# A compact layout for a chunked delta-rule recurrence, and a wide convolution of few tokens by products over overlapping windows, in a one-core decoder kernel

## The chip, the cores and the metric

One core of a Trainium2 chip runs the whole program in one launch. The metric is the device time of that launch in microseconds. The comparison is between the kernel before and the kernel after one change, on the same inputs.

## What is computed

One layer of a hybrid decoder for 512 prompt tokens and 8 samples of 4 tokens (544 columns in all), width 1024, everything in float32: a gated FFN, a mixer with four groups of 256 channels, and a second FFN. Two of the mixer's groups matter here.

```python
# group B: GLU, then a causal depthwise convolution of width 31, LayerNorm, swish
b_conv = causal_dwconv(b_val * sigmoid(b_gate), conv_b, W['b_conv_w'])
# group C (4 heads of 64): delta-rule recurrence over tokens
sa = einsum('bhij,bhj->bhi', S, -kk_t)
S  = S * w_t + sa[..., None] * (kk_t * a_t) + v_t[..., None] * k_t
y_t = einsum('bhij,bhj->bhi', S, r_t)
```

## The kernel before

The activations lie features by tokens. Every large product is three TensorE products of 32-bit halves (`product`, L298 to L308). Its weights come by DMA through SyncE, are split into a high part by ScalarE (`split_hi`, L280) and a low part by VectorE (`split_lo`, L287, the operation of L289). FFN 1 comes first, then the mixer (19 input column blocks, the recurrence, 8 output blocks), then FFN 2. All five engines run programs written out by hand; the order on an engine is the order of the code, and semaphores join them.

**The recurrence.** The 512 prompt tokens are taken in four tiles of 128 (t = 0 to 3), each of two chunks of 64 tokens (c = 0, 1). There are two pairs of heads (p = 0, 1) with two heads each (h = 0, 1). Within a chunk the recurrence becomes the solution of a unit triangular system of 64 x 64 per head, and its inverse is built by doubling blocks of 1, 2, 4, 8, 16, 32 (`LEVELS`). A tile has 13 stages s (`NSTAGE`):

- s = 0: transposes of keys and values (L1118, L1119), taken out by ScalarE into `bv` (L1229).
- s = 1: products of keys with queries and the removal vectors (L1146), for both heads into separate banks. VectorE cuts them by masks into `nib` (L1295), adds the identity (L1299), takes level 0 into `tt_[..,1]` (L1302), and makes `akb` (L1304) and `rbk` (L1305).
- s = 2: transposes of level 0 (L1126), taken out by ScalarE (L1231).
- odd s from 3 to 11: the product `nib` x `tt_` (L1131), masked by VectorE into `xx` (L1310).
- even s from 4 to 12: products of `tt_` with `xx` (L1137 and L1138; at s = 12 only L1138), taken out by ScalarE into `tt_` (L1233) or, at s = 12, into `tf` (L1235). An odd and an even stage are called a level here.

Before the change the two chunks of a tile stand side by side: each of these matrices is 128 x 128 per head, of which only the two diagonal blocks of 64 x 64 are not zero (the product of `akb`, L1157, uses the off-diagonal ones). TensorE multiplies whole 128 x 128 matrices.

Beside a tile t's stages run the seven hops of tile t - 1 (`HOPS`, `chain_pe`: L1173, L1178, L1189, L1198, L1213, L1216), which carry the state from chunk to chunk, and by `BESIDE` the samples' steps q0 to q9, x0, x1 (L1351, L1377, L1404, L1526), splits w2 and w3 of output weights, splits y0 to y3 of the mixer's outputs, and the LayerNorm of group B (b_mean L1415, b_var L1423). PSUM banks 0 to 3 go round as a ring of two pairs (`RING`, `freed`): a stage may write when the stage two places earlier has been read. Behind tile 0's q0 and tile 1's q7 this makes the next stage wait for `rbk` of s = 1.

**The wide convolution.** VectorE does it as 62 taps (31 taps k for two blocks p of channels, `tap`, L975 to L985): one operation of 512 columns for the prompt (L984) and one of 32 for the samples (L985), each adding to `yb`. `fill(n)` (L1759) does the next n taps. It stands behind each input block from m = 15 to 20 (2 taps each) and behind the VectorE part of the odd stages (3 taps each in tile 0, 2 in the others) until the 62 are used up, which is at s = 7 of tile 3. b_mean waits for all taps.

**Start.** ScalarE issues the constants' DMA (`con`, L2017) and two small ones behind it, and waits for all three (L2020) before its squares of x (L436), on which FFN 1's norm rests.

## Time and profile before

| | us |
|---|---|
| median of 3 runs | 1198.92 |
| the three runs | 1193.13, 1198.92, 1202.80 |
| the profiled execution, device time | 1198.65 |
| its span, first to last instruction | 1196.9 |
| TensorE / VectorE / ScalarE / GpSimd busy in it | 1139.4 / 626.6 / 337.0 / 40.7 |
| constants' DMA | 1158.5 KB |

Busy time of TensorE is from a modelled end of each matmul, so 95% busy is not 95% of its peak. Each float32 product of the recurrence is recorded as two matmuls with a weight load each, so an "x8" in a row is four products. In rows of the time line, instructions of one form that follow each other are merged: start, duration from the first's start to the last's end, engine and line, shapes, count, and in brackets the idle time before it with what ended it. TensorE's clock has two levels, 2.4 GHz (shown as 1.00) and 1.2 GHz (0.50).

### The profile page before, as it was taken

To read this page: it belongs to the slowest core of one execution; us is meant where nothing else is said; L and a number is where in the kernel's file an instruction comes from. 1 tells how busy PE (TensorE), PEld (TensorE's weight loads), DVE (VectorE), ACT (ScalarE), POOL (GpSimd) and SP (SyncE) were. 2 spreads that over 40 slices of the span, in tenths; PEclk is the share of its full clock that TensorE was granted. 3 is DMA by queue.
4 is the path that set the end of the run, shared out by engine and by line. 5 is a ranking of instruction groups with operands and counts; after the bars stand their busy time and mean duration, and the time that the engine had idled before them with its cause. 6 is when DMAs were issued, how large, how long until landed. Compare 5 with 4: busy or idle time off the path is not lost.

```text
span 1196.9 us, 21721 instructions
## 1 busy us (share of the span) xinstructions
PE 1139.4 (95%) x8994; PEld 1116.0 (93%) x8994; DVE 626.6 (52%) x1075; ACT 337.0 (28%) x496; POOL 40.7 (3%) x57
## 2 busy tenths in 40 slices
PE   6999999999999997999898999999999999999996
PEld 6999999999999997998787889989999999999996
DVE  5533343333345875889767616785343443344446
ACT  5321222111213433521234343442122221122221
POOL 0000000000000000210221100000000000000001
PEclk9999999999999988999799998899999999999998
DMA  6313232223222211332501002203233232323222
GB/s 223 113 55 105 89 102 74 88 88 100 76 95 79 74 50 53 77 89 76 41 1 36 1 1 73 57 33 106 80 99 104 70 105 71 106 71 105 70 71 75
DMA packets 35391, 92.23 MB, mean 77 GB/s; under 512 B 10368, under 2 KB 12928, under 8 KB 35200
## 3 DMA queue, kind: packets, MB, share of 16 engines
q1 hardware_dynamic: 34320, 88.78, 23.9%
q10 hardware_dynamic: 1008, 2.56, 0.6%
q8 instruction: 45, 0.74, 0.2%
q14 instruction: 18, 0.15, 0.0%
HBM read 88.05 MB, written 3.28 MB: 76 GB/s over the span
## 4 chain that ended last, share of the span: by engine, by line
PE 81%; DVE 12%; ACT 3%; issue 3%; DMA 1%; DVEq 0%; SPq 0%; ACTq 0%
PE ps L306 71%; DVE wl L289 1%; PE ps L1131 1%; DVE mixf L984 1%; PE ps L1137 1%; PE ps L1138 1%; PE ps L367 1%; DVE a L447 1%; ACT wh L284 1%; DVE tb L676 1%; PE ps L376 1%; DMA x<-in_x 1%; DVE xx L1310 1%; DVE mixf L985 1%; PE ps L1573 1%
## 5 line engine op out<-in xcount | busy, mean ns | idle before, releaser
L306 PE MATMUL ps<-xh,wh 128*128 128x272 f32 x1840 | 404.2, 293 | 22.7 <-DVE wl L289 8.8
L306 PE MATMUL ps<-xh,wl 128*128 128x272 f32 x1840 | 400.7, 291 | 0.0
L306 PE MATMUL ps<-xl,wh 128*128 128x272 f32 x1840 | 399.7, 290 | 0.0
L306 PEld LDWEIGHTS ps<-xh,wh 128*128 128x128 f32 x1840 | 299.6, 191 | 25.2 <-DVE wl L289 15.0
L306 PEld LDWEIGHTS ps<-xl,wh 128*128 128x128 f32 x1840 | 299.7, 191 | 0.0
L306 PEld LDWEIGHTS ps<-xh,wl 128*128 128x128 f32 x1840 | 297.9, 191 | 0.0
L284 ACT ACTIVATE wh<-raw 128x1024 fp32r<-128x1024 f32 (+1 forms) x163 | 167.7, 1032 | 319.5 <-PE ps L306 201.2
L289 DVE TENSOR_TENSOR wl<-raw,wh 128x1024 fp32r<-128x1024 f32 (+1 forms) x163 | 192.5, 1202 | 43.6 <-ACT wh L284 43.3
L306 PE MATMUL ps<-hh,wh 128*128 128x272 f32 x704 | 156.8, 289 | 0.0
L306 PE MATMUL ps<-hh,wl 128*128 128x272 f32 x704 | 155.8, 288 | 0.0
L306 PE MATMUL ps<-hl,wh 128*128 128x272 f32 x704 | 155.6, 288 | 0.0
L797 DVE TENSOR_TENSOR h<-silu,ps 128x544 f32<-128x544 f32 x44 | 31.7, 721 | 210.8 <-PE ps L306 208.9
L306 PEld LDWEIGHTS ps<-hl,wh 128*128 128x128 f32 x704 | 114.5, 189 | 0.0
L306 PEld LDWEIGHTS ps<-hh,wh 128*128 128x128 f32 x704 | 114.3, 189 | 0.0
L306 PEld LDWEIGHTS ps<-hh,wl 128*128 128x128 f32 x704 | 114.2, 189 | 0.0
L783 ACT ACTIVATE silu<-silu 128x544 f32<-128x544 f32 x44 | 29.0, 659 | 231.3 <-DVE silu L793 231.3
L793 DVE TENSOR_TENSOR silu<-ps,rb 128x544 f32<-128x544 f32 x44 | 31.8, 724 | 76.9 <-PE ps L306 73.2
L816 DVE TENSOR_TENSOR f<-ps,f 128x544 f32<-128x544 f32 x24 | 17.4, 724 | 75.5 <-PE ps L306 75.5
L984 DVE SCALAR_TENSOR_TENSOR mixf<-zb,par,mixf 128x512 f32<-128x512 f32 x60 | 44.9, 748 | 0.1
L804 DVE TENSOR_TENSOR hl<-h,hh 128x544 f32 (+1 forms) x44 | 31.9, 726 | 4.3
L813 DVE COPY f<-ps 128x544 f32<-128x544 f32 x16 | 11.6, 724 | 42.7 <-PE ps L306 42.7
L1310 DVE TENSOR_TENSOR xx<-ps,con 128x256 f32<-128x256 f32 x40 | 16.7, 422 | 27.0 <-PE ps L1131 26.6
(311 smaller groups left out, 850.5 us busy)
## 6 DMA issues: line engine op xcount, KB each, us to landing
raw<-in_w_gu SPq DMA_DIRECT2D x88, 512.0 KB, 3.7
raw<-in_w_d SPq DMA_DIRECT2D x32, 512.0 KB, 3.6
raw<-in_w_in SPq DMA_DIRECT2D x19, 512.0 KB, 3.5
raw<-in_w_d SPq DMA_DIRECT2D x16, 384.0 KB, 3.0
raw<-in_w_out SPq DMA_DIRECT2D x8, 512.0 KB, 3.6
out_y<-x SPq DMA_DIRECT2D x16, 136.0 KB, 1.7
con<-in_con ACTq DMA_DIRECT2D x1, 1158.5 KB, 5.1
x<-in_x ACTq DMA_DIRECT2D x4, 272.0 KB, 5.6
```

Source lines behind the costliest of these rows:

```text
L284: act.activation(wh[:, s % 4, 0:k, :], raw[:, s % RAW, 0:k, :], ACT.Copy).then_inc(S("w_hi"), 1 + skip)
L289: dve.tensor_tensor(wl[:, s % 4, 0:k, :], raw[:, s % RAW, 0:k, :], wh[:, s % 4, 0:k, :].bitcast(F32), SUB).then_inc(S("w_lo"), 1 + skip)
L306: last = pe.matmul(out[:, n], left[:, s, j], right[:, j, n * H:n * H + H], start=first and opens and j == order[0], stop=final and closes ...
L367: m = pe.matmul(ps[:, 2 * second + h, 3 * i + j:3 * i + j + 1], a3[:, a_, window(3 * h + j)], ones[:, 0:1], start=True, stop=True)
L376: last = pe.matmul(ps[:, 4 + 2 * second + h, P * j:P * j + wide], src[:, 3 * h + j:3 * h + j + 1].to_broadcast([P, P]), ident[:, P - wide: ...
L783: act.activation(silu[:, s % 2], silu[:, s % 2], ACT.Silu).then_inc(S(f"silu{q}"), 1)
L793: dve.tensor_tensor(halves(silu[:, s % 2]), pair(2 * (s % 2)), halves(rb[:]), MUL).then_inc(S(f"gate{q}"), 1)
L797: dve.tensor_tensor(halves(h32[:, s % 2]), halves(silu[:, s % 2]), pair(2 * (s % 2) + 1), MUL).then_inc(S(f"h_mul{q}"), 1)
L804: dve.tensor_tensor(hl[:, j].rearrange(one), h32[:, s % 2], hh[:, j].rearrange(one).bitcast(F32), SUB).then_inc(S(f"h_lo{q}"), 1)
L816: dve.tensor_tensor(halves(f[:, d]), pair(d % 4), halves(f[:, d]), ADD).then_inc(S(f"d_out{q}"), 1)
L984: eng.scalar_tensor_tensor(y1, z1, w, y1, MUL, ADD)
L1310: dve.tensor_tensor(xx[:, p], done(p)[:, 0:2 * P].rearrange(HC, h=2), C_("lev", k=l * P).unsqueeze(1).to_broadcast([P, 2, P]), MUL).then_i ...
```

## The change

1. `nib`, `akb`, `tt_`, `tf` and `xx` become 128 rows by 64 columns per head: chunk c's block stands in its own 64 partitions. The masks shrink with them (`mask` from 384 to 192 columns, `lev` from 768 to 384).
2. Each 128 x 128 product at L1126, L1131, L1137, L1138 and L1157 becomes two products of 64 x 64, on the quarters of the array in which chunk 0 and chunk 1 lie. The transposes of s = 2 become products with the identity.
3. VectorE and ScalarE work on half the columns at L1310, L1231, L1233 and L1235. At s = 1 the cuts into `nib` and `akb` are two operations each on 64 partitions, the identity and level 0 one operation each in place of two, and both parts of `rbk` come last.
4. The taps no longer touch the samples. Their convolution is 10 operations ("windows"): for each block p and each half of the samples a product of 496 columns (4 samples x 4 tokens x 31 taps, read from `zb` with overlap) and a sum over the 31, and two small additions of the bias. They are put between the last taps.
5. `fill` does 3 in place of 2 for m = 17 to 20 and in tile 1. b_mean waits for the windows too. In all 72 items are done: 16 by m = 20, 18, 18, 12 and 8 in tiles 0 to 3.

```diff
-    c[:, CCOL["mask"]:][:, :P] = (s // C == t // C) & (s < t)
-    c[:, CCOL["mask"] + P:][:, :P] = (s // C != t // C) & (s % C < t % C)
-    c[:, CCOL["mask"] + 2 * P:][:, :P] = s % C <= t % C
+    c[:, CCOL["mask"]:][:, :C] = s % C < t[:, :C]
+    c[:, CCOL["mask"] + C:][:, :P] = s % C <= t % C
...
             if k == 0:
-                eng.tensor_scalar(y1, z1, w, par_("bb", p), MUL, ADD)
-                return eng.tensor_scalar(y2, z2, w, par_("bb", p), MUL, ADD)
-            eng.scalar_tensor_tensor(y1, z1, w, y1, MUL, ADD)
-            return eng.scalar_tensor_tensor(y2, z2, w, y2, MUL, ADD)
+                return eng.tensor_scalar(y1, z1, w, par_("bb", p), MUL, ADD)
+            return eng.scalar_tensor_tensor(y1, z1, w, y1, MUL, ADD)
+
+        wide = tmp2[:, 1, 0:NB // 2 * NT * CONVB].rearrange("p (b t k) -> p b t k", b=NB // 2, k=CONVB)
+
+        def windows(eng, n):
+
+            if n >= 8:
+                return eng.tensor_scalar(yb[:, n - 8, DT], yb[:, n - 8, DT], par_("bb", n - 8), None, ADD)
+            n, what = divmod(n, 2)
+            p, h = divmod(n, 2)
+            if what == 0:
+                z = zb[:, p, 542:].rearrange("p (b c) -> p b c", c=34)[:, 4 * h:4 * h + 4, 0:NT]
+                over = bass.AP(z.tensor, z.offset, [list(d) for d in z.ap] + [[1, CONVB]])
+                w = par[:, PCOL["bw"] + p:PCOL["bw"] + 2 * CONVB:2].unsqueeze(1).unsqueeze(1)
+                return eng.tensor_tensor(wide, over, w.to_broadcast([P, NB // 2, NT, CONVB]), MUL)
+            return eng.tensor_reduce(comp(yb[:, p, DT])[:, 4 * h:4 * h + 4], wide, mybir.AxisListType.X, ADD)
...
                 elif s == 2:
                     b = job(p)
-                    pe.wait_ge(S("tt1"), 2 * t + p + 1)
+                    pe.wait_ge(S("tt1"), t + 1)
                     for h in range(2):
-                        last = pe.transpose(b[:, P * h:P * h + P], tt_[:, p, 1, h], ident)
+                        for c in range(2):
+                            last = pe.matmul(b[hp[c], C * h:C * h + C], tt_[hp[c], p, 1, h], ident[hp[c], C * c:C * c + C],
+                                             start=True, stop=True)
...
                     for h in range(2):
-                        last = pe.matmul(b[:, P * h:P * h + P], nib[:, p, h], tt_[:, p, 0, h], start=True, stop=True)
+                        for c in range(2):
+                            last = pe.matmul(b[hp[c], C * h:C * h + C], nib[hp[c], p, h], tt_[hp[c], p, 0, h], start=True, stop=True)
...
                         if s < 12:
-                            pe.matmul(b[:, P * h:P * h + P], tt_[:, p, 1, h], xx[:, p, h], start=True, stop=True)
-                        last = pe.matmul(b[:, 256 + P * h:256 + P * h + P], xx[:, p, h], tt_[:, p, 1, h], start=True, stop=True)
+                            for c in range(2):
+                                pe.matmul(b[hp[c], C * h:C * h + C], tt_[hp[c], p, 1, h], xx[hp[c], p, h], start=True, stop=True)
+                        for c in range(2):
+                            last = pe.matmul(b[hp[c], P + C * h:P + C * h + C], xx[hp[c], p, h], tt_[hp[c], p, 1, h],
+                                             start=True, stop=True)
...
                         k = P * p + C * h
-                        last = pe.matmul(ps[:, 4 + t % 2, k:k + C], akb[:, p, h], bv[:, t % 2, p, 2, C * h:C * h + C],
-                                         start=k == 0, stop=t == 0, skip_group_check=True)
+                        for c in range(2):
+                            last = pe.matmul(ps[rows(c), 4 + t % 2, k:k + C], akb[hp[c], p, h], bv[hp[c], t % 2, p, 2, C * h:C * h + C],
+                                             start=k == 0, stop=t == 0, skip_group_check=True)
...
-                    act.activation(tt_[:, p].rearrange("p k h c -> p (k h c)"), done(p), ACT.Copy).then_inc(S(f"r{s}"), 1)
+                    act.activation(tt_[:, p].rearrange("p k h c -> p (k h c)"), done(p)[:, 0:2 * P], ACT.Copy).then_inc(S(f"r{s}"), 1)
...
+                for c in range(2):
+                    dve.tensor_tensor(nib[hp[c]].rearrange(hik), own(c, "b"), strict[hp[c]].to_broadcast([64, 2, 2, C]), MUL).then_inc(S("near"), 1)
...
+                dve.tensor_tensor(tt_[:, :, 1], nib[:], C_("lev", C).unsqueeze(1).unsqueeze(1).to_broadcast([P, 2, 2, C]), MUL).then_inc(S("tt1"), 1)
+                for c in range(2):
+                    r = hp[1 - c]
+                    dve.tensor_tensor(akb[r].rearrange(hik), own(c, "k"), strict[r].to_broadcast([64, 2, 2, C]), MUL).then_inc(S("ak"), 1)
...
-                fill(2 if t else 3)
+                fill(2 if t > 1 else 3)
...
-                    dve.tensor_tensor(xx[:, p], done(p)[:, 0:2 * P].rearrange(HC, h=2),
-                                      C_("lev", k=l * P).unsqueeze(1).to_broadcast([P, 2, P]), MUL).then_inc(S(f"r{s}"), 1)
-                fill(2 if t else 3)
+                    dve.tensor_tensor(xx[:, p], done(p)[:, 0:P].rearrange(HC, h=2),
+                                      C_("lev", C, l * C).unsqueeze(1).to_broadcast([P, 2, C]), MUL).then_inc(S(f"r{s}"), 1)
+                fill(2 if t > 1 else 3)
...
+            TAPS = [(k, p) for k in range(CONVB) for p in range(2)]
+            for n in range(10):
+                TAPS.insert(2 * CONVB - 9 + 2 * n, (n, None))
...
-                    fill(2)
+                    fill(2 if m < 17 else 3)
```

## Rows read from the trace of the kernel before

**Rows 1.** The page: engines' busy time; the clock granted to TensorE in 40 slices.
```profile
PE 1139.4 (95%) x8994; PEld 1116.0 (93%) x8994; DVE 626.6 (52%) x1075; ACT 337.0 (28%) x496; POOL 40.7 (3%) x57
...
PEclk9999999999999988999799998899999999999998
```

**Rows 2.** Stretches of tiles 0 to 3: length; PE, PEld, DVE, ACT, POOL busy; clock; DMA; GB/s.
```profile
568.10:605.10 37.00, 31.88 (x266) 27.66 (x267) 27.90 (x74) 8.69 (x20) 8.44 (x9) 0.78 0.44 37
605.10:638.50 33.40, 28.93 (x243) 23.61 (x241) 23.13 (x68) 12.56 (x29) 7.93 (x10) 0.95 0.06 17
638.50:665.00 26.50, 24.48 (x208) 21.72 (x209) 20.02 (x47) 12.63 (x26) 4.01 (x6) 1.00 0.06 21
665.00:696.70 31.70, 28.50 (x240) 25.50 (x238) 16.51 (x41) 12.78 (x27) 3.79 (x6) 1.00 0.00 1
```

**Rows 3.** Time line, tile 3: one level of pair 0.
```profile
685.63 0.67 PE L1131 MATMUL ps<-tt,nib 128*128 128x128 f32 x4
...
688.12 0.60 ACT L1233 ACTIVATE tt<-ps 128x512 f32<-128x512 f32 x1 [1.69 <-PE ps L1138]
...
688.81 0.67 PE L1131 MATMUL ps<-tt,nib 128*128 128x128 f32 x4
```

**Rows 4.** Groups by form, 568 to 697 us (the last is the page's).
```profile
L984 DVE SCALAR_TENSOR_TENSOR mixf<-zb,par,mixf 128x512 f32<-128x512 f32 x52 | 38.9, 749 | 0.0
...
L1131 PE MATMUL ps<-tt,nib 128*128 128x128 f32 x160 | 26.1, 304 | 2.0 <-ACT tt L1233 0.9 <-DVE s0t L1526 0.8 <-DVE qnak L1500 0.2
...
L1233 ACT ACTIVATE tt<-ps 128x512 f32<-128x512 f32 x32 | 19.0, 597 | 33.3 <-PE ps L1138 33.3
L1310 DVE TENSOR_TENSOR xx<-ps,con 128x256 f32<-128x256 f32 x40 | 16.7, 422 | 27.0 <-PE ps L1131 26.6
...
L1235 ACT ACTIVATE tf<-ps 128x256 f32<-128x256 f32 x8 | 2.9, 380 | 6.2 <-PE ps L1138 6.1
...
L793 DVE TENSOR_TENSOR silu<-ps,rb 128x544 f32<-128x544 f32 x44 | 31.8, 724 | 76.9 <-PE ps L306 73.2
```

**Rows 5.** Time line: runs of weight loads and products on the whole array and on parts.
```profile
606.39 0.55 PEld L1146 LDWEIGHTS ps<-ar,bt 64*128 64x128 f32 x8 [1.15 <-DVE qtt L1517]
...
607.51 0.54 PEld L1189 LDWEIGHTS ps<-rhs,tf 64*64 64x64 f32 x8
...
615.71 0.32 PEld L1216 LDWEIGHTS ps<-rbk,uv 128*64 128x64 f32 x8
...
629.87 1.08 PE L1404 MATMUL ps<-qex,qbkv 64*64 64x512 f32 x4
...
678.12 0.97 PEld L1131 LDWEIGHTS ps<-tt,nib 128*128 128x128 f32 x8
```

**Rows 6.** Time line of VectorE: a tap and the start of the next; a sample's tap in tile 0.
```profile
671.57 0.74 DVE L984 SCALAR_TENSOR_TENSOR mixf<-zb,par,mixf 128x512 f32<-128x512 f32 x1
...
672.23 0.24 DVE L985 SCALAR_TENSOR_TENSOR mixf<-zb,par,mixf 128x32 f32<-128x32 f32 x1
672.40 0.74 DVE L984 SCALAR_TENSOR_TENSOR mixf<-zb,par,mixf 128x512 f32<-128x512 f32 x1
...
584.85 1.03 DVE L985 SCALAR_TENSOR_TENSOR mixf<-zb,par,mixf 128x32 f32<-128x32 f32 x1
```

**Rows 7.** Groups at the start: the constants' DMA, and ScalarE's wait for the three.
```profile
con<-in_con ACTq DMA_DIRECT2D x1, 1158.5 KB, 5.1
...
17.69 0.66 ACT L436 ACTIVATE a<-x 128x544 f32<-128x544 f32 x1 [4.06 <-DMA dwbd<-in_dw]
```

**Rows 8.** Time line of TensorE: the first transposes of tile 0.
```profile
568.11 0.69 PE L1118 MATMUL ps<-con,kt 128*128 128x128 f32 x2 [2.83 <-DVE mixf L1831]
```

**Rows 9.** Time line of TensorE, tile 1: s = 2 behind q7.
```profile
610.56 0.44 PE L1126 MATMUL ps<-con,tt 128*128 128x128 f32 x2 [1.03 <-DVE rbk L1305]
```

**Rows 10.** Stretches at 1.2 GHz in the recurrence, first and last of three (columns as in rows 2).
```profile
567.70:577.70 10.00, 7.44 (x38) 4.94 (x38) 7.89 (x21) 2.13 (x5) 0.00 (x0) 0.51 1.00 77
...
611.70:615.10 3.40, 3.40 (x17) 2.85 (x15) 2.53 (x7) 0.92 (x3) 0.00 (x0) 0.50 0.00 0
```

More of the change, by code:

```diff
@@ L68 @@
 _n = 0
-for _name, _k in (("ident", P), ("ones", P), ("hb", P), ("mask", 3 * P), ("lev", 6 * P), ("scan", N), ("cnt", 32),
+for _name, _k in (("ident", P), ("ones", P), ("hb", P), ("mask", C + P), ("lev", 6 * C), ("scan", N), ("cnt", 32),
                   ("wcol", 2), ("eps", 3), ("smask", 64), ("slev", 64), ("bsel", 8), ("idc", 64)):
@@ L1290, in part @@
                     return done(h).rearrange(quads, i=2, c=2, w=2)
-                def mask(n):
-                    return C_("mask", P, n * P).rearrange(HC, h=2).unsqueeze(1).to_broadcast([P, 2, 2, C])
-                for h in range(2):
-                    dve.tensor_tensor(nib[:, :, h].rearrange(ick, c=2), part(h)[:, :, :, 0], mask(0), MUL).then_inc(S("near"), 1)
-                idb = ident.unsqueeze(1).to_broadcast([P, 2, P])
-                for p in range(2):
-                    dve.wait_ge(S("near"), 2 * t + 2)
-                    dve.tensor_tensor(nib[:, p], nib[:, p], idb, ADD).then_inc(S("unit"), 1)
@@ L1300, in wkv_dve @@
-                for p in range(2):
-                    dve.wait_ge(S("unit"), 2 * t + p + 1)
-                    dve.tensor_tensor(tt_[:, p, 1], nib[:, p], C_("lev").unsqueeze(1).to_broadcast([P, 2, P]), MUL).then_inc(S("tt1"), 1)
-                for h in range(2):
-                    dve.tensor_tensor(akb[:, :, h].rearrange(ick, c=2), part(h)[:, :, :, 0], mask(1), MUL).then_inc(S("ak"), 1)
-                    dve.tensor_tensor(rbk[:, t % 2, :, h].rearrange(ick, c=2), part(h)[:, :, :, 1], mask(2), MUL).then_inc(S("r1"), 1)
@@ L1306, in wkv_dve, with own @@
-                fill(2 if t else 3)
+                def own(c, kind):
+                    two = ps[hp[c if kind == "b" else 1 - c], 2 * (place(("r", t, 1)) % 2):2 * (place(("r", t, 1)) % 2) + 2]
+                    return two.rearrange("p h (i c w k) -> p h i c w k", i=2, c=2, w=2)[:, :, :, c, 0]
+                hik = "p i h k -> p h i k"
+                strict = C_("mask", C).unsqueeze(1).unsqueeze(1)
+                upto = C_("mask", P, C).rearrange(HC, h=2).unsqueeze(1).to_broadcast([P, 2, 2, C])
```

42 lines of the change are left out of this document (28 added, 14 removed).

## The prediction

> **What bounds the kernel now.** I began with the page. TensorE is busy in nearly the whole span, and the only slices in which it is granted much less than the full clock lie in the middle [rows 1]. The change touches only that middle (the mixer), and the start through the constants. The split into stretches then gives the four tiles of the recurrence: 37.0, 33.4, 26.5 and 31.7 us, 128.6 together, 11% of the time [rows 2]. VectorE is busy for 27.9 of 37.0 us in tile 0 and 16.5 of 31.7 in tile 3, TensorE for 24.5 of 26.5 in tile 2. So no engine bounds it alone: it is a chain of TensorE, VectorE, TensorE, ScalarE which two pairs of heads share, with taps in front of VectorE's part and hops in front of TensorE's. A quiet level shows the bare chain: from one L1131 of pair 0 to the next 3.18 us (685.63 to 688.81) [rows 3]. It is the product 0.67, the mask 0.42, four products and their latency about 1.05, the copy 0.60, some 0.15 of hand-overs, and 0.27 in which pair 1's L1131 holds TensorE. In the groups, VectorE's idle time before `xx` is put to L1131 (26.6 us), ScalarE's before `tt` to L1138 (33.3 us): each waits for TensorE's products [rows 4].
>
> **The price of a product.** A run of n records of d each that lasts T has a pitch of (T - d)/(n - 1). For L1131 (whole array, 128 columns) that is (0.97 - 0.19)/7 = 0.111 us; for L1189 (one quarter, always the same within a run, 64 columns) (0.54 - 0.135)/7 = 0.058; for L1216 (column halves in turn, 64 columns) (0.32 - 0.135)/7 = 0.03; for L1146 (row halves in turn, 128 columns) (0.55 - 0.19)/7 = 0.05, half of what 128 columns cost otherwise [rows 5]. So column halves work side by side, and row halves too, where they write to different banks. L1404 shows column halves side by side within one bank: four records of 512 columns in 1.08 us [rows 5], where 0.111 x 4 = 0.44 us each, one after another, would be 1.8. The change has neighbours that differ in both, and write to one bank on different partitions. No row of before shows that. The ends are 0.03 and 0.058 us a record; I take 0.03, since both halves of the case are seen overlapping.
>
> The Trainium skill (TensorEngine Tiling, section Restrictions and Gotchas, Gotcha 1) says that different row tiles can't access the same PSUM bank simultaneously. No row of before has that case. By it the quarters would go one by one, and the sum would be the first rival's.
>
> With 0.03: an odd stage (L1131, both pairs) goes from 8 records x 0.111 = 0.89 us to 16 x 0.03 = 0.48, saving 0.41; an even stage from 16 x 0.111 = 1.78 to 32 x 0.03 = 0.96, saving 0.82; L1157 from 0.9 to 0.48, saving about 0.45. The mask falls from 256 to 128 columns: 0.42 for 256 and 0.72 for 544 [rows 4] lie on a line that gives 0.28 for 128 (no less than half, 0.21, no more than 0.42). The copy falls from 512 to 256 columns, 0.60 to 0.38 [rows 4]. A level's chain becomes 0.43 + 0.28 + 0.67 + 0.38 + 0.2 of hand-overs, about 2.0 us, for 3.18.
>
> **Taps.** A tap takes 0.83 us from start to start (671.57 to 672.40), its large part 0.66 of it (to 672.23) [rows 6]. So a tap becomes 0.66. A window's product or sum, 496 columns, isn't in the trace: between 0.33 and 1.3 (half and twice the 0.66 that 496 columns have by the 0.72 for 544 [rows 4]). I take 0.66, by L984 of 512 columns; eight of them lie in tiles 2 and 3, where VectorE has room, so even 1.3 costs at most a few us. Three items and two masks are 2.0 + 0.56 = 2.55 us of VectorE a level (3 x 0.83 + 0.84 = 3.3 before), two items 1.9 (2.5 before).
>
> **The change part by part** (minus is gained):
>
> - Start. The constants shrink by 576 columns, 288 of 1158.5 KB. In proportion to their 5.1 us that is 1.3 us of the wait of 4.06 [rows 7]; with the small DMAs behind it I take -1.0 (0 to -1.3).
> - Input blocks. TensorE's first transposes of tile 0 sit idle for 2.83 us behind VectorE's last block [rows 8]: VectorE sets the end there. m = 16 has two taps, -0.33; m = 17, 18 and 19 have three of 0.66 for two of 0.83, +0.33 each. Sum +0.7.
> - Tile 0, start: s = 1 has 8 VectorE operations for 10 and `rbk`'s first is the seventh for the eighth: -0.35.
> - Tile 0, levels: VectorE bounds s = 3, 9 and 11 at 3.3 us and more; each gives 0.75, -2.3. At s = 5 a sample's tap takes 1.03 us for 0.24 (GpSimd works at that time) [rows 6]; it goes, as one more does: -1.5 (-0.5 to -2.4). At s = 7 TensorE is at 1.2 GHz and bounds the level; products at double price, (0.41 + 0.82) x 2 less what VectorE's 2.55 us put in their place: -2.2. Sum -6.0.
> - Tile 1: the products of s = 2 wait for `rbk` behind q7 [rows 9]; both parts of it come two operations earlier, -0.7. Then TensorE bounds until s = 7: -0.8 (s = 3, at 1.2 GHz), -0.82, -0.45, -0.41, -0.82. From there on VectorE bounds it (split w2, two updates of the samples' state, masks and taps): masks -0.9, taps at 3 x 0.66 for 2 x 0.83 +1.05. Sum -3.85.
> - Tile 2: VectorE lies in front of s = 3 (-0.55 for s = 1's fewer operations, -0.33 for taps). s = 4 gives 0.82 + 0.45, s = 5 and 6 give 0.41 + 0.82. The next two levels fall from 3.2 to 2.6, where VectorE's 1.9 and a split of 0.71 set the end; the last gives 0.8. Sum -5.4.
> - Tile 3: start and s = 3, -0.65 (0.2 of the gain goes to the wait for the state's copy), then -1.27 and -1.23 as before, two bare levels -1.2 each, -0.4 at s = 11. Behind b_mean the LayerNorm of group B is the path and doesn't change. Sum -5.95.
> - Changes between whole array and parts: none is priced by a row. I bound one at nothing and at a weight load's 0.135 to 0.19 us that the next run doesn't hide [rows 5], and take 0.17 for two more a tile in three tiles, +1.0 (0 to +4, at eight a tile).
> - Clock. At present 20 us of the recurrence run at 1.2 GHz, in three stretches of which the first has 10.0 and the last 3.4 us, behind gaps or behind many tiny products [rows 10]. TensorE gets more gaps now. I take one and a half of such short stretches more, each some 1.7 us dearer: +2.5 (-2 to +8 within this case).
>
> Sum: -1.0 + 0.7 - 0.35 - 6.0 - 3.85 - 5.4 - 5.95 + 1.0 + 2.5 = -18.35. From the profiled execution's 1198.65 (span 1196.9 and 1.75 around it; the runs' median is 1198.92) that is 1180.3; I say 1181. This case's own range is 1173 to 1189.
>
> **Rivals.**
>
> *The quarters take turns* (0.058 a record). An odd stage then costs 0.93 us for 0.89, an even one 1.86 for 1.78: TensorE gains nothing. What is left is VectorE's and ScalarE's part: tile 0 -3.9, tile 1 -0.7, tile 2 -1.6, tile 3 -0.45, with start, input blocks and changes of shape +0.7 - 1.0 + 1.0: -5.95, 1193. For it speaks that no row shows two row halves in one bank; against it L1404 and L1146 [rows 5].
>
> *TensorE falls to 1.2 GHz now and again.* Its streaming within a level halves, in levels shortened by a third. In a tile with hops what it has left is about 6.7 us of levels, 5.8 of hops and 2.5 of the rest, 15 us, which at 1.2 GHz become 30. One part in three of tiles 1 to 3 at that clock adds 15, and in place of my 2.5: 1181 + 12.5 = 1194.
>
> *TensorE stays at 1.2 GHz for most of the recurrence: slower.* Place: tiles 1 to 3, TensorE's own part. Price: 3 x 15 = 45 us, tile 0 some 7 more (it is hidden there in part by 2.55 us of VectorE a level), less 3 that VectorE hides in tile 1: about +47 for the 2.5, 1226. It decides the sign once somewhat under half of the tiles is cold. For it speaks that the clock stayed low from 567.7 to 577.7 although TensorE was busy for 7.4 us of the 10 [rows 10], with transposes and row halves among its work. Against it: it came back within 3.4 us in tile 1, where products of whole levels and hops filled it [rows 10], and tiles 2 and 3 stay at 1.00 with TensorE busy for 24.5 of 26.5 us and 28.5 of 31.7 [rows 2]. The Trainium skill (TensorE: Matmul & The Clock Gate, Part 1) has the throttled state as the default, released by activity; the rows on both sides agree, and none of them shows how quarters count.
>
> *The change doesn't save what it says on VectorE:* a product over overlapping windows or a sum at 1.3 us in place of 0.66 adds 8 x 0.64 = 5 us of VectorE in tiles 2 and 3, of which perhaps 3 show: 1184. It lies in the first case's range.
>
> **How the numbers follow.** Likeliest 0.63 (with the last rival in it), turns 0.19, now and again cold 0.12, cold for the most 0.06. One per cent, about what a measurement of this kernel can tell from no change, is 12 us: faster than that is below 1187. Of the likeliest case, 0.85 lies there, of the third about 0.1: 0.55. Above 1211 only the last case: 0.06. The rest, 0.39, is within 1%. The range takes in turns and the middle of the third case: 1173 to 1197; 1 in 10 lies below or just outside the first case, 1 in 10 above.
>
> **What would show it.** Runs of the quarter products of 16 records: a pitch of 0.03 says I am right, 0.058 the first rival. A bare level of 2.0 us from one L1131 of pair 0 to the next in tile 3; 2.9 or 3.2 says no. Tiles of about 30.5, 29.5, 21 and 26 us; the wait for the constants near 3.0 us; TensorE's idle time before tile 0's transposes grown by 0.7. A clock below 1.00 over tiles 2 and 3 would speak for the cold cases. I would be wrong if the levels shortened and the hops took their place as the chain, or if the windows' operations stood in front of `xx`.

## The result, and the profile after

The changed kernel takes 1195.68 us (median of 20 runs, 1190.76 to 1203.65). The kernel before takes 1203.89 us in the same measurement (20 runs, 1193.13 to 1210.77). The ratio is 0.9937, with a 95% interval of 0.9915 to 0.9958: 0.6% faster, about 7.6 us, where 18 were forecast. The profiled execution has a span of 1195.4 us and a device time of 1197.13. That is 1.5 us above the median of its kernel, while the profiled execution of the kernel before (1198.65) is 5.2 us below the median of its own, so whole times are compared here by the runs, and profiles only stretch by stretch. Three later runs that took over 1.5% longer than the fastest of their kernel (two of e3, one of e9) are left out of the ratios and clocks below.

The page, to hold against [rows 1]:

```profile
PEclk9999999999999998999766989889999999999998
```

The recurrence lies in the 20th to 23rd of the 40 slices. The 21st and 22nd (598 to 658 us) stand at 6, where both stood at 9 in the kernel before. The stretches of the four tiles, each from its first transposes to those of the next, the last to the product for b_mean (columns as in rows 2):

```profile
569.60:603.40 33.80, 27.12 (x394) 23.52 (x394) 24.23 (x55) 6.59 (x20) 7.67 (x9) 0.68 0.43 40
603.40:635.00 31.60, 27.39 (x377) 21.27 (x375) 23.63 (x53) 9.84 (x27) 8.73 (x10) 0.72 0.07 18
635.00:663.10 28.10, 25.86 (x343) 21.34 (x342) 17.28 (x42) 11.20 (x28) 4.13 (x6) 0.67 0.07 20
663.10:682.60 19.50, 17.79 (x330) 15.03 (x326) 10.42 (x27) 7.87 (x23) 3.20 (x6) 1.00 0.01 3
```

The bounds in rows 2 were round ones, so here are the same stretches of the kernel before, cut in the same way:

```profile
568.10:604.60 36.50, 31.38 (x262) 27.16 (x262) 27.40 (x73) 8.56 (x20) 8.44 (x9) 0.78 0.45 37
604.60:636.80 32.20, 28.95 (x246) 23.86 (x244) 21.94 (x61) 11.76 (x28) 7.93 (x10) 0.95 0.06 18
636.80:664.90 28.10, 24.86 (x212) 21.87 (x211) 21.62 (x56) 13.53 (x29) 4.01 (x6) 1.00 0.05 20
664.90:690.20 25.30, 23.39 (x204) 20.88 (x203) 14.83 (x39) 9.71 (x23) 3.79 (x6) 1.00 0.01 2
```

Read the last two numbers before the DMA share together with the length. Tile 3 has a granted clock of 1.00 in both kernels and falls from 25.3 to 19.5 us. Tiles 1 and 2 had 0.95 and 1.00 before, have 0.72 and 0.67 now, and give 0.6 us and nothing. Tile 0 went from 0.78 to 0.68 and gives 2.7 us. TensorE is no less busy in tile 2 (25.86 us for 24.86), though the level products that it has there should take about half as long at the full clock: the lower clock took that back.

One level of tile 3, against [rows 3]:

```profile
679.81 0.92 PE L1146 MATMUL ps<-tt,nib 64*64 64x64 f32 x16
...
681.82 0.92 PE L1146 MATMUL ps<-tt,nib 64*64 64x64 f32 x16
```

The bare chain is 2.01 us from one product of a level to the next, for 3.18. A run of weight loads on the diagonal quarters, and the groups, against [rows 4, 5]:

```profile
677.80 0.54 PEld L1146 LDWEIGHTS ps<-tt,nib 64*64 64x64 f32 x16
```

```profile
L1252 ACT ACTIVATE tt<-ps 128x256 f32<-128x256 f32 x32 | 12.2, 384 | 28.7 <-PE ps L1155 27.7
L1337 DVE TENSOR_TENSOR xx<-ps,con 128x128 f32<-128x128 f32 x40 | 10.7, 288 | 26.0 <-PE ps L1146 25.3
L996 DVE TENSOR_TENSOR mixf<-zb,par 128x496 f32<-128x496 f32 x4 | 2.7, 664 | 0.0
L997 DVE TENSOR_REDUCE mixf<-mixf 128x16 f32<-128x496 f32 x4 | 2.6, 656 | 0.0
```

The pitch is (0.54 - 0.135)/15 = 0.027 us. The mask of 128 columns takes 0.288, the copy of 256 takes 0.384, a product or sum over windows 0.66 us. All the prices of instructions are as forecast.

What was not forecast is how long the clock stays low. The two long stretches, and what stands before each on TensorE's time line:

```profile
584.90:615.70 30.80, 30.26 (x343) 26.29 (x342) 19.68 (x47) 7.44 (x23) 4.67 (x6) 0.50 0.01 2
629.50:653.50 24.00, 20.56 (x191) 16.57 (x193) 13.76 (x38) 6.14 (x15) 0.79 (x2) 0.50 0.11 37
```

```profile
585.44 0.58 PE L1369 MATMUL ps<-ar,bt 64*32 64x64 f32 x4 [3.31 <-issue]
...
588.13 5.42 PE L1378 MATMUL ps<-ar,s0t 64*64 64x8 f32 x61
...
631.45 0.98 PE L1146 MATMUL ps<-tt,nib 64*64 64x64 f32 x13 [2.57 <-DVE s0t L1554]
```

TensorE stood still for 3.31 us with no releaser in the profile ("issue"), and then went on at 1.2 GHz for 30.8 us, though it was busy for 30.26 of them. The second stretch begins in a wait of 2.57 us behind VectorE's update of the samples' state. I add up such time from slices of 1 us, as twice what the granted clock lacks to 1: between 560 and 725 us the kernel before has 31 us at 1.2 GHz, the changed one 68. The 20 runs say the same without a trace: their mean granted clock is 0.9515, and that of the kernel before, measured beside e1 and beside e5 below, 0.965 and 0.966. A difference of 0.014 over 1195 us is 2 x 0.014 x 1195 = 33 us more at 1.2 GHz. Measured side by side (e5) the difference is 0.016, or 38 us.

### The profile page after: what moved, and what is told of

Its sections match the earlier page's. It is cut to its first block, busy times and chain, and to the rows that moved or that the text cites. A ratio compares the mean times of both kernels' runs of the same rounds, so it can differ in the third digit from the quotient of the medians.

```text
span 1195.4 us, 22718 instructions
## 1 busy us (share of the span) xinstructions
PE 1134.6 (95%) x9522; PEld 1108.9 (93%) x9522; DVE 617.1 (52%) x1015; ACT 328.9 (28%) x496; POOL 40.3 (3%) x57
## 4 chain that ended last, share of the span: by engine, by line
PE 82%; DVE 11%; issue 3%; ACT 2%; DMA 1%; DVEq 0%; SPq 0%; ACTq 0%
PE ps L306 71%; DVE mixf L982 2%; DVE wl L289 1%; PE ps L1146 1%; PE ps L367 1%; DVE a L447 1%; ACT wh L284 1%; PE ps L376 1%; PE ps L1153 1%; PE ps L1155 1%; DVE tb L676 1%; PE ps L1197 1%; DMA x<-in_x 1%; PE ps L1164 1%; PE ps L1601 1%
## 5 line engine op out<-in xcount | busy, mean ns | idle before, releaser
L306 PE MATMUL ps<-xh,wh 128*128 128x272 f32 x1840 | 405.7, 293 | 22.4 <-DVE wl L289 8.8
L306 PE MATMUL ps<-xh,wl 128*128 128x272 f32 x1840 | 401.9, 292 | 0.0
L306 PE MATMUL ps<-xl,wh 128*128 128x272 f32 x1840 | 400.7, 291 | 0.0
L306 PEld LDWEIGHTS ps<-xh,wh 128*128 128x128 f32 x1840 | 301.5, 192 | 24.9 <-DVE wl L289 14.9
L306 PEld LDWEIGHTS ps<-xl,wh 128*128 128x128 f32 x1840 | 301.1, 192 | 0.0
L306 PEld LDWEIGHTS ps<-xh,wl 128*128 128x128 f32 x1840 | 299.0, 192 | 0.0
L306 PE MATMUL ps<-hh,wh 128*128 128x272 f32 x704 | 156.8, 289 | 0.0
L306 PE MATMUL ps<-hh,wl 128*128 128x272 f32 x704 | 155.7, 288 | 0.0
L306 PE MATMUL ps<-hl,wh 128*128 128x272 f32 x704 | 155.6, 288 | 0.0
L306 PEld LDWEIGHTS ps<-hl,wh 128*128 128x128 f32 x704 | 114.5, 189 | 0.0
L306 PEld LDWEIGHTS ps<-hh,wh 128*128 128x128 f32 x704 | 114.2, 189 | 0.0
L306 PEld LDWEIGHTS ps<-hh,wl 128*128 128x128 f32 x704 | 114.2, 189 | 0.0
L1337 DVE TENSOR_TENSOR xx<-ps,con 128x128 f32<-128x128 f32 x40 | 10.7, 288 | 26.0 <-PE ps L1146 25.3
```

Source lines behind the costliest of these rows:

```text
L306: last = pe.matmul(out[:, n], left[:, s, j], right[:, j, n * H:n * H + H], start=first and opens and j == order[0], stop=final and closes ...
```

## Experiments

"Recurrence" is, in the profiled execution, the time from tile 0's first transposes to the product for b_mean; "cold" is the time at 1.2 GHz between 560 and 725 us, as above. "Clock" is the mean over a kernel's runs, with that of the kernel before, measured beside it, in brackets: read the two together, since the latter alone moves from 0.965 to 0.970. The ratios are to the kernel before on the same chip. Recurrence and cold are of one execution each, and the two profiles of the changed kernel differ by 4.3 us in the first; e3's profiled execution (1214.61 us) is far above the 1201 us that its ratio stands for.

| run | ratio (95% interval) | clock | recurrence | cold |
|---|---|---|---|---|
| before (profile) | 1 | 0.965 to 0.970 | 122.1 | 31 |
| changed (profile) | 0.9937 (0.9915 to 0.9958) | 0.952 | 113.0 | 68 |
| e5, changed, again | 0.9926 (0.9897 to 0.9956) | 0.950 (0.966) | 108.7 | 65 |
| e1 fillers | 0.9893 (0.9831 to 0.9955) | 0.964 (0.965) | 104.5 | 17 |
| e2 stores late | 0.9882 (0.9826 to 0.9938) | 0.950 (0.965) | 111.9 | 75 |
| e3 other order of quarters | 0.9949 (0.9912 to 0.9987) | 0.949 (0.965) | 128.0 | 85 |
| e4 taps only | 1.0017 (0.9985 to 1.0048) | 0.963 (0.965) | 121.7 | 23 |
| e6 fillers, state first | 0.9880 (0.9847 to 0.9913) | 0.965 (0.966) | 110.3 | 34 |
| e7 fillers on before | 1.0051 (1.0026 to 1.0075) | 0.967 (0.966) | 127.9 | 17 |
| e8 compact only | 0.9935 (0.9909 to 0.9962) | 0.950 (0.966) | 106.5 | 48 |
| e9 items moved | 0.9897 (0.9858 to 0.9936) | 0.957 (0.970) | 97.5 | 31 |
| e10 items and fillers | 0.9907 (0.9879 to 0.9935) | 0.966 (0.970) | 108.9 | 31 |
| e11 quarter fillers | 0.9906 (0.9875 to 0.9938) | 0.963 (0.970) | 105.4 | 31 |
| e12 fewer fillers | 0.9841 (0.9805 to 0.9877) | 0.967 (0.970) | 101.1 | 24 |
| e13 items 2, few fillers | 0.9738 (0.9692 to 0.9784) | 0.972 (0.965) | 97.4 | 20 |
| e14 items 2 | 0.9875 (0.9824 to 0.9925) | 0.953 (0.965) | 104.7 | 51 |
| e15 few fillers on before | 0.9977 (0.9948 to 1.0006) | 0.969 (0.965) | 119.6 | 20 |
| e16 items 2, fewest | 0.9781 (0.9730 to 0.9832) | 0.966 (0.965) | 97.4 | 24 |
| e17, e13 again | 0.9763 (0.9713 to 0.9814) | 0.970 (0.965) | 98.1 | 20 |
| e18 and stores late | 0.9775 (0.9726 to 0.9824) | 0.968 (0.965) | 93.8 | 17 |

### Is it the clock, and does it come from the waits?

**e1, fillers.** Products whose result nobody reads, in front of TensorE's work of chosen stages (50 over tiles 0 to 3, and one ahead of each head's products with the samples' state of each pair). They write to a part of a PSUM bank that is not used otherwise.

```diff
+        def fill_pe(pe, n, seen=0):
+            if n and seen > 0:
+                pe.wait_ge(S("y_out"), seen)
+            for _ in range(n):
+                pe.matmul(ps[:, 7, 256:384], ident, con[:, CCOL["lev"]:CCOL["lev"] + P], start=False, stop=True, ...)
...
+            fill_pe(pe, FILLERS.get((t, s), 0), t if s > 6 else max(t - 1, 0))
             for p in range(2):
                 if s == 0:
```

> The kernel after, with useless whole-array products (128 x 128 by 128 columns, into spare columns of bank 7) on TensorE in front of the stages at which it waits: some 35 in tile 0, 20 in tile 1, 6 in tiles 2 and 3, and four within q3. About 60 of 0.22 us are 13 us more work of TensorE, half of it in waits. Clock theory (the missing gain is TensorE at 1.2 GHz for some 60 us of the recurrence, where it was 20): the stretches at 1.2 GHz in 568 to 700 us shrink to under 30 us in sum and the time falls below the kernel after's by 2 to 12 us, to a ratio of 0.980 to 0.992 against before. VectorE theory (taps, split and samples' state on VectorE took the gain, the clock is a side effect): the time is equal to after's or up to 8 us longer, ratio 0.994 to 1.001, even if the clock rises.

Measured 0.9893. The interval from 4 runs reaches from a gain of 0.4% to 1.7%. The profile is clearer: 17 us cold for 68, and tiles 1 and 2 are what they should have been.

```profile
608.90:636.50 27.60, 26.54 (x419) 21.14 (x415) 21.83 (x51) 9.62 (x28) 7.87 (x10) 1.00 0.07 21
636.50:659.00 22.50, 19.89 (x356) 16.52 (x350) 17.95 (x43) 11.31 (x29) 4.13 (x6) 1.00 0.09 26
```

They take 27.6 and 22.5 us for 31.6 and 28.1. Tile 0 didn't shorten (34.9 for 33.8).

**e7, the same fillers on the kernel before**, as the control.

> The kernel before with the same useless products (at the same places of its levels), to see whether they help by themselves. The kernel before has 20 to 31 us at 1.2 GHz between 560 and 725 us. Clock theory: there is little to win back, the products add about 60 records of 0.11 to 0.22 us, partly in waits, so between -0.3% and +0.3%. Rival (such products help any version of this kernel, by filling TensorE in a part where it is throttled anyway): -0.5% or better, as much as they give the changed kernel.

1.0051: they cost the kernel before 0.5%, above what I expected. The changed kernel gains 0.3 to 0.4% by them (e1 against e5 and the first measurement), which alone lies inside the intervals. The two together are 0.9%, with a noise of some 0.7 by the intervals of the runs compared: clear of it, though not by much. So they are no good in themselves; what they win back belongs to the levels of the compact layout.

**e11, quarter fillers.** Each product of the whole array is replaced by two on the diagonal quarters.

```diff
+                for c in range(2):
+                    pe.matmul(ps[hp[c], 7, 256:384], ident[hp[c], C * c:C * c + C], con[hp[c], ...], ...)
```

> The first experiment with each useless whole-array product (two records of about 0.11 us) replaced by two on diagonal quarters, of the same 128 columns, side by side: the same count of places and TensorE busy about as long, with half of the array. If it is TensorE's idle time in the waits that lets the clock fall, these hold it as well as the whole-array ones: 0.989, clock 0.96. If it is the quarters themselves that leave the clock low however busy TensorE is, the clock stays near 0.950 and the ratio at 0.993 or above.

0.9906, in time no different from e1's 0.9893. The clock lies between the two cases: 0.006 below that of the kernel before beside it, for 0.001 in e1 and 0.016 in e5, with 31 us cold. So products on quarters win back over half of the clock, and the shape of the new products isn't all that keeps it down; that it plays some part isn't ruled out.

**e3, the order of the quarters.** Both heads of one chunk, then both of the other; otherwise the changed kernel.

```diff
-                    for h in range(2):
-                        for c in range(2):
+                    for c in range(2):
+                        for h in range(2):
                             last = pe.matmul(b[hp[c], C * h:C * h + C], nib[hp[c], p, h], ...)
```

> The kernel after with the quarter products in another order, all of chunk 0 and then all of chunk 1, so that neighbours within a job mostly use the same quarter. If neighbours on different quarters work side by side and those on the same one take turns, the pitch of the weight loads rises from 0.03 to near 0.058 us, a bare level of tile 3 from 2.0 to about 2.8 us. Clock theory: TensorE is denser and may keep 2.4 GHz longer, so that the time is within 3 us of after's, ratio 0.991 to 0.997. VectorE theory: levels bound by VectorE hide it in tiles 0 and 1, tiles 2 and 3 pay 5 to 8 us, ratio 0.997 to 1.001.

```profile
694.45 0.33 PE L1153 MATMUL ps<-xx,tt 64*64 64x64 f32 x4
694.57 0.33 PE L1154 MATMUL ps<-tt,xx 64*64 64x64 f32 x4
694.74 0.33 PE L1153 MATMUL ps<-xx,tt 64*64 64x64 f32 x4
```

Eight records take 694.74 - 694.45 = 0.29 us, a pitch of 0.036, for 0.029 in the changed kernel. So turning from quarter to quarter with each product is worth only 0.2 us in an even stage; in the odd stages no difference shows (16 loads in 0.59 to 0.60). The pitch of 0.058 that I expected didn't come, and a bare level takes 2.29 us (699.19 to 701.48) where I expected 2.8. This profile also holds the price of the clock, by chance: tile 2 was at 1.2 GHz from end to end.

```profile
642.80:678.40 35.60, 33.65 (x344) 29.10 (x342) 18.37 (x44) 11.51 (x28) 3.72 (x6) 0.50 0.05 16
```

Tile 2 has the same work in the changed kernel and, but for four fillers, in e1. It takes 35.6 us at a clock of 0.50, 28.1 at 0.67 and 22.5 at 1.00. Some 2 us of the first may be the order of the quarters (five even stages of 0.2, doubled at 1.2 GHz), which leaves 11 for a whole tile. In the kernel before the tile took 28.1 us at 1.00. So with two thirds of the tile at 1.2 GHz the loss of 5.6 us is all that the layout gives there.

### Which half of the change gives what?

**e4, the taps alone**: the kernel before with the windows, one large tap an item, and three items a level in tiles 0 and 1. **e8, the compact layout alone**: the changed kernel with the taps and counts of the kernel before.

> The kernel before with only the taps' part of the change: prompt taps of 512 columns alone, the samples by ten window operations, three items in place of two for m = 17 to 20 and in tile 1. By the prediction's steps: input blocks +0.7, tile 0 -1.4 for its VectorE-bound levels and -0.5 to -2.4 at s = 5, tile 1 between 0 and +1, tile 2 -0.33 and the like: 1 to 4 us faster than before, ratio 0.997 to 0.9995. Clock theory: TensorE's stretches at 1.2 GHz are as before's, some 20 us. Should it bring 7 us by itself, the compact layout brings nothing.

> The compact layout alone, with the taps, the samples' convolution and the number of items a level as in the kernel before. My terms for the two halves: the layout carries nearly all of the gain (products, masks, copies), the taps nothing (the converse experiment gave 1.0017). Clock theory: within 0.3% of the changed kernel in this call, ratio 0.991 to 0.997, clock as low as the changed kernel's. Rival (VectorE's items decide in tiles 0 and 1, and the shorter levels only pay with the windows): 0.998 or more.

1.0017 and 0.9935, the latter against 0.9926 for the whole change beside it (**e5**). The taps' part is worth nothing that can be measured (I had expected 0.05 to 0.3%), the layout all of it.

> The changed kernel once more, beside the next three, as their yardstick. In the first measurement its 20 runs had a mean granted clock of 0.9515 and a ratio of 0.9937; I expect the same here, about -0.6% (-7.6 us) against the kernel before, and a clock that is at least 0.010 lower than that of the kernel before in the same call. If the clock of the two kernels is alike in this call, my theory (the clock took what the products gave) falls.

e5 repeats the result, with a clock of 0.950 for the 0.966 of the kernel before. e8, with the layout alone, has 0.950 too.

### What is VectorE's?

**e9, items moved**: the same taps and windows, given out in another order. **e14** takes them out of tile 0's level 5 as well.

```diff
+        ITEMS = [(3, 3, 3, 3, 3, 3), (3, 3, 3, 2, 1, 1), (3, 3, 2, 2, 2, 2), (3, 3, 3, 3, 3, 0)]        # e9
+        ITEMS = [(3, 3, 1, 3, 3, 3), (3, 3, 3, 2, 2, 1), (3, 3, 3, 2, 2, 2), (3, 3, 3, 3, 3, 0)]        # e14
-                fill(2 if t > 1 else 3)
+                fill(ITEMS[t][s // 2])
...
-                    fill(2 if m < 17 else 3)
+                    fill(2)
```

> The changed kernel with VectorE's items given out otherwise: two a step in the input stage (12 for 16), three a level in tile 0, then 3, 3, 3, 2, 1, 1 in tile 1 and 3, 3, 2, 2, 2, 2 in tile 2, and three a level in tile 3 (15 for 8). TensorE's wait before tile 0 (3.52 us behind VectorE's last block) falls by up to 4 x 0.66 = 2.6 us; tile 1, where VectorE bounds the last levels, gives up to 3; tile 3 loses about 2, since three items and two masks are 2.5 us where its bare level is 2.0. Sum -2 to -4 us against the changed kernel, so about 0.990 of the kernel before. Clock theory adds: the clock stays as low as in the changed kernel (0.950). Rival (VectorE's items in tiles 0 and 1 are where the missing 11 us are): 0.985 or better.

> The same order of items without useless products. Against the first order of moved items (0.9897) TensorE's wait of 2.56 us behind the samples' masks in tile 0 goes or falls under 0.5 us: 0.9875. The clock stays between the changed kernel's and the one before: 0.955 to 0.960. Rival (that wait is only filled by the level's own chain, which is late by then too): 0.9897, no change.

0.9897 and 0.9875, as expected. TensorE's wait before tile 0 falls from 3.52 to 1.58 us, and in tile 1 that behind the samples' state from 2.57 to 1.24. e9's profile has 31 us cold for 65 to 68 and e14's has 51, but the runs show little of it: their clocks are 0.012 below that of the kernel before beside them, where e5's was 0.016 below. In e14's profile TensorE's idle time without a releaser stands at 3.35 us, and the clock falls behind it. It took the place of the wait that the moved items were to remove: with one item at level 5 VectorE was through at 584.82 and then stood still for 2.98 us behind TensorE's products.

Why level 5 of tile 0: this is VectorE and GpSimd in the kernel with fewer fillers (e12).

```profile
587.17 3.96 DVE L982 SCALAR_TENSOR_TENSOR mixf<-zb,par,mixf 128x512 f32<-128x512 f32 x3
```

```profile
586.64 3.94 POOL L1513 TENSOR_TENSOR qex<-qbkv,con 32x512 f32<-32x512 f32 x3 [0.18 <-POOL uv L1298]
```

Three taps take 3.96 us beside GpSimd's work, and 2.07 without it (583.53, same kernel). TensorE waited 2.47 us behind them. It isn't the DMA traffic of that time: in e6, where the DMA engines were busy for 0.01 of 585 to 590 us, three taps beside GpSimd took 4.51.

### Do both together reach the forecast?

**e12**, e1 with 32 fillers instead of 54, kept where TensorE waits longest; **e15**, the same set on the kernel before; **e13**, the set with e14's order of items; **e17**, e13 once more; **e16**, as e13 with 18 fillers.

```diff
-        FILLERS = {(0, 2): 6, (1, 2): 1, (2, 2): 4, (3, 2): 2, (0, 3): 1, (0, 4): 2, (0, 5): 4, ...
+        FILLERS = {(0, 2): 6, (0, 5): 4, (0, 6): 1, (0, 8): 1, (0, 10): 1, (0, 12): 1, (1, 2): 1, (1, 9): 3, (1, 11): 8, (2, 2): 4, (3, 2): 2}   # e12, e13, e15, e17, e18
+        FILLERS = {(0, 2): 6, (1, 9): 2, (1, 11): 4, (2, 2): 4, (3, 2): 2}                                                                        # e16
```

> The first experiment with 28 useless products for 50 or so: those in front of the samples' products of their state and in most levels of tiles 0 and 1 are left out, those in the longest waits kept (behind the masks of each tile, tile 0's level 5, tile 1's levels 9 and 11). On the kernel before the full set cost 0.5%, so about a quarter of a per cent is to be saved if the clock holds: 0.987. If the many small ones were what held the clock, it falls to about 0.955 and the ratio is 0.992.

> The smaller set of useless products on the kernel before. They add 28 x 2 records where the full set added some 55 x 2 and cost 0.5%; the kernel before has the better clock already. Clock theory: 0.999 to 1.003. Rival (they help either kernel alike): 0.995 or better.

> The changed kernel with the smaller set of useless products (0.9841 alone) and the items moved again: one item in place of three at tile 0's level 5, where GpSimd's work doubles the time of a tap, the two going to later tiles. Moved items alone gave 0.9897, the products 0.9841, the changed kernel 0.9926 to 0.9937. If waits of VectorE and TensorE's clock are two causes, the gains add: 0.978 to 0.982, and the recurrence takes 96 to 99 us (101.1 and 97.5 us with one of them each). If they are one (fewer waits keep the clock up, and nothing else is lost), it is no better than 0.984.

> As the first of these four with 18 useless products for 28 or so: none in tile 0's levels, two and four in tile 1's levels 9 and 11. If the products pay where TensorE waits longest (behind the masks and behind the samples' state), this is as good as the larger set, within 0.2%; if those in tile 0 matter, its clock falls under 0.962 and it loses 0.3% or more.

> The same kernel as e13_items2_few_fillers once more. If its 0.9738 stands: 0.971 to 0.979, clock 0.970. If it was a lucky draw, it lands at the sum of its parts, 0.9841 and 0.9875 for 0.993: 0.979 or above.

e12 gives 0.9841, and 0.9977 on the kernel before: of 1.6%, some 0.2% (0.5% by the end of its interval) is what such products do for either kernel. Against the changed kernel's 0.9926 to 0.9937 they win 0.9%, which is 0.6 to 0.7% more than on the kernel before, with some 0.5 of noise. This is the strongest sign that the clock took the gain: nothing but useless work was added, and with it the changed kernel is 1.4% faster than the kernel before with the same products, where I had forecast 1.5. (The larger set holds 32, not the 28 of my expectations.) e13 gives 0.9738 and its repeat 0.9763. By e12's and e14's gains over the changed kernel (0.85% and 0.5% against 0.9926) the sum would be 0.979; both lie slightly below it, so the two gains add, as expected. e16 (0.9781) is the same within the intervals. The tiles of e13 take 29.4, 25.3, 22.7 and 20.0 us, the last three at a granted clock of 1.00. In e13, e17 and, on the kernel before, e15 the clock is 0.004 to 0.007 above that of the kernel before beside them.

**e10** has the first order of items and the full set of fillers.

> The same order of items together with the useless whole-array products of the first experiment. Clock theory: the two add, 0.989 of the first experiment less 0.3%: 0.984 to 0.988 of the kernel before, clock 0.96 or more, the shortest recurrence so far (about 102 us). Rival (both attack the same waits): no better than 0.989.

It fell short of the 0.984 to 0.988 that I expected: 0.9907, no better than either alone. Its tile 0 took 37.9 us (e9: 29.5). The full set has fillers in most of tile 0's levels and in front of each head's products with the samples' state; e12 and e13 leave most of these out. Which of them did it wasn't taken apart; that profile also has a cold stretch of 17 us in tile 0.

### The stores

**e2** moves the four stores of group B behind the recurrence; **e6** does this with e1's fillers and loads the samples' state ahead of group A's stores; **e18** does it with e13.

```diff
             sp.dma_start(s0t[:], a["s0"]).then_inc(S("in_s0"), 16)
-            sp.wait_ge(S("glu"), 2)
-            zs = zb[:, :, 542:].rearrange("p i (b c) -> p i b c", c=34)
-            for i in range(2):
-                sp.dma_start(o["o_b"][:, i, 0:30], zb[:, i, 512:542]).then_inc(S("out"), 16)
-                sp.dma_start(o["o_b"][:, i, 30:].rearrange("p (b c) -> p b c", c=30), zs[:, i, :, 4:]).then_inc(S("out"), 16)
             for m in range(4, KD):
                 load(sp, MIX0, 0, OUT0 + m, a["w_out"][m], KD)
+            sp.wait_ge(S("glu"), 2)
...
             sp.wait_ge(S("c_s"), NC_)
```

> The kernel after, with the four stores of the wide convolution's state (out_o_b, many small packets) issued at the end of the recurrence in place of its start. Fetch theory (TensorE's 3.3 us without work and without a releaser in tile 0 is its instruction load behind these stores, and it starts the long stretch at 1.2 GHz): the hole goes, the low clock from 585 to 615 us shrinks or moves, and the time falls 3 to 8 us, ratio 0.987 to 0.991 against before. Rival (the hole is of that one execution, or has another cause): ratio 0.992 to 0.996, as after's.

> The changed kernel with the useless whole-array products of the first experiment, the samples' state loaded ahead of the small stores of group A, and the stores of group B moved behind the recurrence. Clock theory: the granted clock returns to that of the kernel before (0.96 or more) and the recurrence (first transposes to b_mean) takes about 103 us, for 113.0 in the changed kernel and 104.5 with the products alone; the idle time of TensorE before the samples' products of their state (1.33 us behind the load with the products alone) is gone. Time -1.2% to -1.5% (1189 to 1193 for a kernel before of 1207). Rival (the gain was lost to engines other than TensorE, and the first experiment's 0.9893 is chance): within 0.2% of the changed kernel in this call, whatever the clock.

> The same with the stores of group B (4 DMAs, 270 KB in packets of 120 bytes and more) moved behind the recurrence. If they are what TensorE's unexplained idle time and its wait for the samples' state come from, both are under 0.5 us and the time falls by 1.5 to 3.5 us against the repeat. If the idle time stays, the stores of group A or something else are behind it, and only the wait for the state (1.8 us) goes: -1 to -2 us or, where other work fills it, nothing.

e2's profile still has 2.3 us of TensorE without a releaser and 75 us cold; the interval of its 0.9882 takes in the 0.9926 and the 0.9937 of the changed kernel, so the time decides nothing. In 590 to 592 us of e2's profile the DMA engines were busy for 0.10 of the time, and TensorE stood still all the same. e6 is 0.9880, as e1, but its recurrence took 110.3 us where I expected 103: tile 0 took 39.5, with TensorE 2.80 us behind the samples' masks. e18 has no idle time without a releaser, and 0.70 us behind the load of the state (e13 1.84, e17 0.61). Its recurrence is the shortest (93.8), and the time is that of e17 (0.9775 for 0.9763): in that kernel the stores cost nothing that shows in the whole.

## Why the prediction was wrong

The measured 1195.68 us lie inside the whole range of 1173 to 1197, which was made to take in two of the rivals, and outside this case's own 1173 to 1189. The gain of 7.6 us is less than half of the 18.35 of the sum.

**The prices were right.** A pitch of 0.027 to 0.029 us for the quarters (forecast 0.03, and the first rival's 0.058 falls), 2.01 us for a bare level (2.0), 0.288 and 0.384 for mask and copy (0.28 and 0.38), 0.66 for a window (0.66). By the Trainium skill (TensorEngine Tiling, Restrictions and Gotchas, Gotcha 1) row tiles can't use one PSUM bank at once; these runs of products in one bank don't agree with it, and the measurement decides.

**Tile 3 was right**, -5.95 forecast and 25.3 - 19.5 = 5.8 found. It is the tile at the full clock.

**Tiles 1 and 2 were right at that clock and wrong in the run.** With fillers they take 27.6 and 22.5 us, 4.6 and 5.6 less than before, for 3.85 and 5.4. In the changed kernel they give 0.6 and 0.

**The step that failed is the term of the clock**: "TensorE gets more gaps now. I take one and a half of such short stretches more, each some 1.7 us dearer: +2.5". In its place the time at 1.2 GHz between 560 and 725 us grew by 37 us, in stretches of 24 and 31 us where I had counted on ones of 3.4. Against e1's, tiles 1 and 2 alone lost 4.0 + 5.6 = 9.6 us to it. I had argued from [rows 10] that the clock comes back within 3.4 us where TensorE is filled by products of whole levels. But the change itself takes those away. The second rival had the mechanism and supposed a third of tiles 1 to 3 at 1.2 GHz. It was 0.28 x 2 of tile 1, 0.33 x 2 of tile 2 and nothing of tile 3, so 18 + 19 of 79 us, near a half. For it I had 1194, and its chance (0.12) was too low. That this number lies so near the measured one is in part luck: at its price of 15 us a tile a half would be some 21 us, and tiles 1 and 2 lost 9.6. The Trainium skill (TensorE: Matmul & The Clock Gate, Part 1) has the low clock as the default state, which activity releases. The stretch from 584.90 to 615.70 bears out the first half and not the second: it stayed at 0.50 throughout, with TensorE busy by the records for 30.26 of 30.80 us.

**Why the clock stayed low so long isn't shown.** A rival to the waits is the idle time without a releaser in tile 0. Every profile of the compact layout without fillers has it but e9's, which also has the least cold time (31 us for 48 to 85). It doesn't account for all: the second stretch of the changed kernel begins at 629.50 us behind VectorE, and e5's first runs from 570 to 605 us at 0.51, where that idle time begins only at 586.8.

**Tile 0 was wrong for two reasons.** I forecast -6.35 and found -2.7. One is the clock (0.68 for 0.78): the samples' products of their state, 64 small ones, took 5.7 us for 3.83 (588.75, kernel before). The other is a step: I let the gain of 1.5 us at level 5 stand on the sample's tap of 1.03 us that goes. It went, and GpSimd slowed the large taps instead, up to 1.53 us each where 0.92 was the most before. The three items took 4.38 us (from 582.38), and 4.43 in the kernel before (584.00 to 588.43), so the step gave nothing. What that wait cost by itself isn't shown: e14, without two of those items, is within the intervals of e9, and its profile has the idle time without a releaser in its place.

**The ends.** The input blocks are right: 3.52 - 2.83 = +0.7. The wait for the constants gave 4.1 - 3.6 = 0.5 of the 1.0. Behind b_mean the twenty small products of b_var fell into a cold stretch and took 3.97 us for 2.36 (+1.6), which no step had. In the profiled executions the recurrence is 9.1 us shorter, but the span only 1.5: 1.5 us went before tile 0, of which the two ends above are 0.2, and 6.0 behind the product for b_mean. Most of the latter is chance: between 725 and 875 us the changed kernel's profile has 20.5 us at 1.2 GHz for 10.2, by one stretch (776.50 to 786.70) among the large products of L306, which are the same in both kernels. The profiles of e4 and e7, which have the old layout, and of e17 have such a stretch, and those of e5 and e13 haven't.

Whether the clock is the whole of the missing 11 us can't be told to the microsecond. Over the runs of the kernel before (11 to 27 beside each group of experiments), the span falls by 9 to 11 us for each 0.01 of mean clock, and by 7 over the changed kernel's 20. For the difference of 0.014 to 0.016 that is 10 to 18 us. No run kept the clock up without adding work.

## What to carry to other kernels

When a change halves the work of an engine that is granted its clock, ask what the engine does between the pieces that remain: the time at the lower clock belongs into the sum as the largest unknown, not as a small term, and a tile that was at 1.00 before is no evidence that it will be. Compare the granted clock of the same stretch in both profiles before looking for any other cause, and take a second profile: here one kernel's two differed by 4.3 us in the recurrence. The waits to remove first are those in front of TensorE, by giving out VectorE's side work by where it has room; a few useless products belong only into waits that can't be removed, and a control on the kernel before tells whether they do what they are thought to.

## What the runs showed of the hardware

- Products on diagonal quarters that write to one bank, on different partitions, run side by side: 0.027 to 0.029 us a record where the quarter changes with each product, 0.036 with two products in a row on a quarter (e3), and 0.058 in a run that stays on one ([rows 5], L1189).
- TensorE stood still for 1.9 to 5.3 us, with no releaser, at the samples' first products in the changed kernel, e2, e3, e5, e8 and e14. DMA engines were busy with small packets (0.23 MB in 1704 packets between 582.2 and 585.4 us of the changed kernel), and one packet of each of two instruction queues falls into that time. The small packets are neither needed nor enough: with the stores of group B gone (e2) 2.3 us of it stayed at a DMA share of 0.10, and e9 has 2433 packets between 582 and 588 us and none of it. With the fillers (e1, e6) and in e18 there was none either. At other products 0.3 to 2.5 us of it stand in e4, e11, e13, e16 and e17. The cause is open.
- GpSimd's work nearly doubles a tap on VectorE (0.69 to 1.3 us from start to start, e12), and whatever stands in that level inherits it.
- Tile 2 of the recurrence, with the same work but for four useless products in e1 and another order of the quarters in e3, took 22.5 us at a granted clock of 1.00 (e1), 28.1 at 0.67 (changed) and 35.6 at 0.50 (e3).
